# The second norm's transposes in another order, the first chunk's squares and the third chunk's loads moved up, and a padding of 512 bytes

## What is computed

```python
u = rmsnorm(h, mix_norm_g)
q, k, v, o_pre, if_pre = split(u @ w_in)
# per head, chunk by chunk, with a running state (c_st, n_st, m_st):
num = w_inter * (q @ c_st) + scores @ v          # scores = (q k^T) * exp(log_d - m_t)
den = w_inter * (q . n_st) + sum(scores)
o = _rms(num / max(|den|, exp(-m_t))) * norm_g   # head by head
h = h + (o * sigmoid(o_pre)) @ w_out
u = rmsnorm(h, ffn_norm_g)
h = h + (silu(u @ w_gate) * (u @ w_up)) @ w_down  # w_gate, w_up: 1024 x 2816
```

## Time and profile before

| | us |
|---|---|
| median of 3 runs | 2248.97 |
| lowest, highest | 2247.64, 2250.45 |
| profiled execution | 2248.88 |
| its span in the trace | 2247.2 |

### The profile page before, as it was taken

How to read it: one execution, slowest core, us unless ns; L and a number is a source line. 1 busy time by engine, 2 the same in 40 slices (tenths; PEclk the granted TensorE clock), 3 DMA queues, 4 the chain that set the end, 5 groups by cost and what they waited for, 6 DMA issues and landing times.

```text
span 2247.2 us, 29481 instructions
## 1 busy us (share of the span) xinstructions
PE 2169.3 (97%) x10440; PEld 1779.8 (79%) x10440; DVE 1459.4 (65%) x2274; ACT 922.8 (41%) x1670; POOL 282.3 (13%) x373
## 2 busy tenths in 40 slices
PE   5999989989999999999989999799899999999999
PEld 4788878878888888888868888688688888888887
DVE  8765467786656565578677644667765656656764
ACT  4433653344333333345434346433433333333443
POOL 4111111120101010100112111111210100100000
PEclk9999999999999999999999999999999999999999
DMA  4333354213232323863414334532123233257443
GB/s 142 99 113 108 105 214 141 85 47 113 99 112 89 107 95 133 300 220 113 150 61 136 99 99 146 206 132 76 55 97 108 96 102 101 93 200 239 146 128 107
DMA packets 200289, 281.56 MB, mean 125 GB/s; under 512 B 12913, under 2 KB 131697, under 8 KB 200177
## 3 DMA queue, kind: packets, MB, share of 16 engines
q1 hardware_dynamic: 171696, 183.07, 25.4%
q0 software_dynamic: 28480, 97.02, 12.3%
HBM read 197.73 MB, written 82.31 MB: 125 GB/s over the span
## 4 chain that ended last, share of the span: by engine, by line
PE 87%; DVE 7%; issue 2%; DMA 2%; ACT 2%; SPq 0%; POOL 0%; DVEq 0%; ACTq 0%; POOLq 0%
PE ps L2163 13%; PE ps L2165 13%; PE ps L2166 13%; PE ps L1912 7%; PE ps L1916 6%; PE ps L1914 6%; PE ps L2209 6%; PE ps L2213 6%; PE ps L2211 6%; PE ps L1825 2%; PE ps L1826 2%; PE ps L1827 2%; PE ps L1832 1%; DMA vtc<-proj_hbm 1%; PE ps L2082 1%
## 5 line engine op out<-in xcount | busy, mean ns | idle before, releaser
L1666 DVE TENSOR_TENSOR ring<-raw_f,ring 128x512 fp32r<-128x512 f32 x308 | 211.4, 687 | 196.8 <-ACT ring L1103 196.3
L1103 ACT CAST ring<-raw_f 128x512 fp32r<-128x512 f32 x308 | 190.4, 622 | 215.4 <-PE ps L2166 200.5
L2163 PE MATMUL ps<-u_lo,ring 128*128 128x512 f32 x704 | 277.6, 394 | 0.0
L2165 PE MATMUL ps<-u_hi,ring 128*128 128x512 f32 x704 | 276.1, 392 | 0.0
L2166 PE MATMUL ps<-u_hi,ring 128*128 128x512 f32 x704 | 275.8, 392 | 0.0
L2209 PE MATMUL ps<-ring,ring 128*128 128x512 f32 x616 | 244.4, 397 | 3.0 <-DVE ring L1744 2.9
L2213 PE MATMUL ps<-ring,ring 128*128 128x512 f32 x616 | 243.5, 395 | 0.0
L2211 PE MATMUL ps<-ring,ring 128*128 128x512 f32 x616 | 243.5, 395 | 0.0
L2163 PE MATMUL ps<-t_op,ring 128*128 128x512 f32 x528 | 208.7, 395 | 6.2 <-DVE ring L1666 6.2
L2166 PE MATMUL ps<-t_op,ring 128*128 128x512 f32 x528 | 209.0, 396 | 0.0
L2165 PE MATMUL ps<-t_op,ring 128*128 128x512 f32 x528 | 208.6, 395 | 0.0
(11 more groups left out here) (219 smaller groups left out, 4263.7 us busy)
## 6 DMA issues: line engine op xcount, KB each, us to landing
...
```

The lines of the kernel that those rows point to most:

```text
L1103: nc.scalar.copy(four(ring[slot][:, 0, :]), feed_source(q, s)).then_inc(w_hi_done, 1)
L1666: nc.vector.tensor_tensor(four(ring[slot][:, 1, :]), feed_source(q, s), four(ring[slot][:, 0, :].bitcast(F32)), ALU.subtract).then_inc(w_l ...
L2163: pe.matmul(banks(bank), wh, moved(kind, 1, k), start=(fresh and k == 0), stop=False, skip_group_check=True)
L2165: pe.matmul(banks(bank), wh, moved(kind, 0, k), start=False, stop=False, skip_group_check=True)
```

## The change

Ten edits, in the order of the diff.

1. The twelve pair units of the second norm come in the order of a new list: part B and A of all pairs first, part C (T4) of all pairs last.
2. The area `r_q` gets a padding of 512 bytes in place of 128, and the third output buffer moves with it; the areas behind it (`r_a`, `r_b`, `r_c`) move by 384 bytes.
3. SP loads `vtc` and `qkc` of chunk 2 right after the gates of chunk 0, ahead of the gates of chunk 1 and of the two pieces of `w_out`; the gain comes between these.
4. POOL squares chunk 0's numerators before it waits for the last store of the projections, sets the ones and loads the first residual.
5. `split_out(1, k)`: ACT does k 0 to 3 together after the head scales of chunk 1; VectorE does four together after `add_out` in chunks 1 and 2.
6. VectorE does the sums of pair 0 ahead of `hg_low(7)`, and `add_out(7, 0)` behind units 0 and 1, `add_out(7, 1)` ahead of unit 3's low pass.
7. ACT and VectorE do the ring slots of q 4 to 6 ahead of the T4 units and the last four units between the passes of the first group.
8. The last output tile is cut 6 + 2 instead of 4 + 4 around unit 3.
9. On TensorE units 13, 14, 15 stand in the middle of q 4, 5 and 6 instead of ahead of q 4.
10. q 4 waits for 10 units, q 6 for 12, q 12 for all.

```diff
@@ -54,2 +54,5 @@
 
+SECOND_UNITS = [("B", 0), ("A", 0), ("B", 1), ("A", 1), ("B", 2), ("B", 3), ("A", 2), ("A", 3), ("C", 0), ("C", 1),
+                ("C", 2), ("C", 3)]
 GATE_DVE = (0, 0, 8, 9, 10, 11, 12, 13, 14, 18)
@@ -151,3 +154,3 @@
         r_v = region(TILES * HEADS * VW * 4)
-        r_q = region(32 * KB + P)
+        r_q = region(32 * KB + 512)
         r_a = region(16 * KB)
@@ -193,3 +196,3 @@
         num = place("num", r_c + 28 * KB, [P, HEADS, VW], F32)
-        hg_at = [r_q, r_q + 8 * KB, r_q + 24 * KB + P]
+        hg_at = [r_q, r_q + 8 * KB, r_q + 24 * KB + 512]
         hg_hi = [place(f"hg_hi{s}", at, [P, KD, P], F32R) for s, at in enumerate(hg_at)]
@@ -400,6 +403,6 @@
         def part_of(stage, n):
-            return FIRST_UNITS[n - 4][0] if stage % 2 == 0 else "BAC"[(n - 4) % 3]
+            return (SECOND_UNITS if stage % 2 else FIRST_UNITS)[n - 4][0]
 
         def pair_of(stage, n):
-            return FIRST_UNITS[n - 4][1] if stage % 2 == 0 else (n - 4) // 3
+            return (SECOND_UNITS if stage % 2 else FIRST_UNITS)[n - 4][1]
 
@@ -567,8 +570,11 @@
                 load_og(0)
+                load_vtc(2)
+                load_qkc(2)
                 load_og(1)
+                load_wo(1, 0)
                 sp.wait_ge(colt_turned, h + 1)
                 sp.dma_start(gain2[:, :], ffn_norm_g[0:1, :].partition_broadcast(P)).then_inc(gain_loaded, 16)
-                load_wo(1, 0)
                 load_wo(1, 1)
-                for c in range(2, TILES):
+                load_og(2)
+                for c in range(3, TILES):
                     load_qkc(c)
@@ -730,6 +736,2 @@
 
-                pool.wait_ge(p_stored[1], h * 384 + 384)
-                nc.gpsimd.memset(v1[1][:, :, DV:VW], 1.0).then_inc(ones_set, 1)
-                pool.wait_ge(p_fed, h * PU + PU)
-
                 def load_res(q):
@@ -740,4 +742,2 @@
 
-                load_res(0)
-
                 def squares(c):
@@ -749,3 +749,7 @@
                         .then_inc(sq_done, 1)
-                    if 1 <= c < 4:
+                    if c == 0:
+                        pool.wait_ge(p_stored[1], h * 384 + 384)
+                        nc.gpsimd.memset(v1[1][:, :, DV:VW], 1.0).then_inc(ones_set, 1)
+                        pool.wait_ge(p_fed, h * PU + PU)
+                    if c < 4:
                         load_res(c)
@@ -1075,5 +1079,5 @@
                         act.wait_ge(p_fed, h * PU + PU)
-                    if c in (1, 2):
-                        split_out(1, 4 * c - 4)
-                        split_out(1, 4 * c - 3)
+                    if c == 2:
+                        split_out(1, 4)
+                        split_out(1, 5)
                     if c >= 3:
@@ -1086,5 +1090,4 @@
                     head_rstd(c)
-                    if c in (1, 2):
-                        split_out(1, 4 * c - 2)
-                        split_out(1, 4 * c - 1)
+                    for k in ((), range(0, 4), range(6, 8))[c] if c < 3 else ():
+                        split_out(1, k)
 
@@ -1120,3 +1123,3 @@
                 feed_hi(0, 3)
-                for n in range(5, OP_UNITS):
+                for n in range(5, 10):
                     op_hi(st + 1, n)
@@ -1128,6 +1131,8 @@
 
-                first_kept(0)
-                first_kept(1)
                 feed_hi(0, 4)
+                first_kept(0)
                 feed_hi(0, 5)
+                first_kept(1)
+                op_hi(st + 1, 10)
+                op_hi(st + 1, 11)
                 feed_hi(0, 6)
@@ -1198,2 +1203,4 @@
                             feed_hi(n, q + RING)
+                            if isinstance(n, int) and n == 0 and q < 4:
+                                op_hi(st + 1, 12 + q)
                         elif not last:
@@ -1634,4 +1638,4 @@
                     if c in (1, 2):
-                        split_out(1, 4 * c - 2)
-                        split_out(1, 4 * c - 1)
+                        for k in range(4 * c - 4, 4 * c):
+                            split_out(1, k)
 
@@ -1677,2 +1681,3 @@
                 gate_heads(7)
+                sum_early(st + 1, 0)
                 hg_low(7)
@@ -1680,12 +1685,11 @@
                 add_out(6, 1)
-                sum_early(st + 1, 0)
                 sum_early(st + 1, 1)
                 norm2_rows(6)
-                add_out(7, 0)
                 op_lo(st + 1, 0)
                 op_lo(st + 1, 1)
+                add_out(7, 0)
                 sum_early(st + 1, 2)
                 op_lo(st + 1, 2)
-                op_lo(st + 1, 3)
                 add_out(7, 1)
+                op_lo(st + 1, 3)
                 op_lo(st + 1, 4)
@@ -1695,12 +1699,13 @@
                 sum_early(st + 1, 3)
-                for n in range(6, 10):
-                    op_lo(st + 1, n)
+                op_lo(st + 1, 6)
+                op_lo(st + 1, 7)
                 feed_sums(0, 2)
-                for n in range(10, 14):
-                    op_lo(st + 1, n)
+                op_lo(st + 1, 8)
                 feed_sums(0, 3)
-                for n in range(14, OP_UNITS):
-                    op_lo(st + 1, n)
-                for q in range(4, RING):
-                    feed_lo(0, q)
+                op_lo(st + 1, 9)
+                feed_lo(0, 4)
+                feed_lo(0, 5)
+                op_lo(st + 1, 10)
+                op_lo(st + 1, 11)
+                feed_lo(0, 6)
 
@@ -1797,2 +1802,4 @@
                             feed_lo(n, q + RING)
+                            if isinstance(n, int) and n == 0 and q < 4:
+                                op_lo(st + 1, 12 + q)
                         elif not last:
@@ -2136,5 +2143,5 @@
                 out_tile(7, 0, 0, KD)
-                out_tile(7, 1, 0, 4)
+                out_tile(7, 1, 0, 6)
                 turn_unit(st + 1, 3)
-                out_tile(7, 1, 4, KD)
+                out_tile(7, 1, 6, KD)
                 turn_unit(st + 1, 4)
@@ -2184,8 +2191,10 @@
                         if first and q == 4:
-                            turn_unit(st + 1, 13)
-                            turn_unit(st + 1, 14)
-                            turn_unit(st + 1, 15)
-                            pe.wait_ge(op_lo_done, (st + 1) * OP_UNITS + OP_UNITS - 2)
+                            pe.wait_ge(op_lo_done, (st + 1) * OP_UNITS + 10)
                         if first and q == 6:
-                            pe.wait_ge(op_lo_done, (st + 1) * OP_UNITS + OP_UNITS - 1)
+                            pe.wait_ge(op_lo_done, (st + 1) * OP_UNITS + 12)
+                        if first and 4 <= q < 7:
+                            feed(n, q, b, 0, 2)
+                            turn_unit(st + 1, 9 + q)
+                            feed(n, q, b, 2, 4)
+                            continue
                         if first and q == 12:
```

6 lines of the change are left out of this document (3 added, 3 removed).

## The result

The kernel after runs in 2194.68 us (median of 4 runs, 2191.05 to 2198.51), before in 2248.3: a ratio of 0.9761, with a 95% interval from 0.9742 to 0.9781. The forecast was 2216.8 us with a range from 2207 to 2229, so the direction was right, the time lies outside the range, and 22 us of gain were not foreseen. The profiled execution took 2195.8 us, its span is 2194.1.

The account below looks back on a forecast made before the run. The prediction took TensorE, busy for 2169.3 of 2247.2 us, as the bound, with only its gaps to gain. Terms of -1.6, -3.1 and -11.4 gave -16.1 us per half, -32.2 in all: 2216.8 us, range 2207 to 2229.

Parts of the forecast that it names:

- What bounds the kernel: Whole kernel: TensorE is busy for 2169.3 of 2247.2 us, so little but its gaps can be had.
- Chunk 0, POOL: Chunk 0's head rows: POOL's squares start 2.5 us earlier, the transposes 2.1; 0.5 lost to low clock; -1.6 us per half.
- Chunk 2's values: Chunk 2: the values' earlier load removes TensorE's 3.28 us wait, but VectorE limits the gain; -3.1 us per half.
- Both together: Chunk stage: the gains from POOL's earlier squares and the values' earlier load, 4.7 us per half.
- The second norm: Second norm to q = 7: reordered work removes waits of 2.70 and 3.12 us and low clock; -11.4 us per half.
- Padding: Moved areas of rings, weights and T2/T3 operands: no effect on products, 1 us either way over the program.
- Sum: Whole program: -16.1 us per half, -32.2 in all, from 2248.97 to 2216.8 us.
- the first: Rival, chunks: VectorE is the bound there too and nothing of their 4.7 us arrives; 2226 us, chance 0.12.
- second: Rival, second norm: VectorE's queue slips by new collisions with POOL, taking half of 11.4 us; 2228 us, chance 0.11.
- the fourth: Rival, q 0 to 6: the clock stays down throughout, slower than before; 2249 us and up, at most 2273, chance 0.03.
- fifth: Rival, whole change: no effect, because a load or store was late, not the order; 2245 to 2250 us, chance 0.05.
- the third: Rival, short gaps: the clock dips once or twice more per half, 1.5 to 2.6 us each; up to 2227, chance 0.07.

## Why the prediction was wrong, by its steps

**What bounds the kernel:** right. TensorE's gaps were the place to look; that the products themselves could come faster was not asked.

**Chunk 0, POOL (-1.6):** the head rows came 2.1 us earlier and the gap is 4.3, as worked out. What it is worth hangs on the values' load (alone: nothing) and on where the clock is low; on top of the loads the traces have 0.35 and 2.0 us, the medians 0.8 for both halves, where 3.2 were forecast. So this term's size is not confirmed.

**Chunk 2's values (-3.1):** right, 3.15 and 3.29 alone. VectorE is the bound as counted: 13.9 us were worked out from the end of chunk 1's outputs to the outputs of chunk 2, and the trace of after has 325.89 - (310.08 + 2.05) = 13.8.

**Both together (-4.7):** 5.9 and 5.4 without the padding, 3.8 and 3.7 with it. The difference is mostly the clock. The weights' wait of 1.85 us did stay, but in after TensorE is granted 1.2 GHz, the lower of its two levels, for 3.4 us behind it, and in the kernel without the padding it is not: there the same product lasts 0.47 us, here 0.77. (In the first half the low stretch around chunk 0's head rows is also 3.4 us there and 6.8 here.) TensorE had run at full clock before both, and the gap is the same (1.86 and 1.85), so what decides between the two is not shown. The prediction said that a gap of 1.80 alone leaves the clock up, from one row. The Trainium skill, "TensorE: Matmul & The Clock Gate", section "A second HAM failure mode: psum-queue depth-cycling", which it weighed against that and gave 0.07, tells of a kernel in which frequent short idling between groups of products made the clock go down and up; by this stretch, the trace of after agrees, once per half, and that of the kernel without the padding does not. In the second norm, where it was feared, the granted clock is 1.00 from 467.7 to 503, and there the forecast holds.

**The second norm (-11.4):** right, 11.6 and 11.5, with the waits of 1.11 (forecast 1.3) and 0.55 (0.6), none before unit 3, none before q = 4.

**Padding (0, 1 us either way): this step failed,** and it alone put the time out of the range. It compared the mean durations of products with the T2/T3 operands and with the inputs, 395 and 394 ns, and took one for moved and the other for unmoved. Both means mix slots of both areas, and the first also holds the products on T4, which is not moved, so each holds slow and fast products in about the same share (229.6 and 229.8 ns from start to start over a group of the feed); what differs is the pair, not the operand. And the bound didn't follow even so: there are 7560 products of 512 columns in the feeds, drains and projections, so 1 ns in the mean is 7.6 us, not under 1. The gain in the traces, 53.1 - 31.5 = 21.6 us, is 2.9 ns per product. The row that would have shown it is in the same trace: steps of the same feed group at 8.37 us for 36 products and 10.89 for 48.

**Sum.** 2248.97 - 32.2 = 2216.8 is nearly the time of the kernel without the padding, 2218.5, in part by differences that cancel, as said with that kernel. The rivals: the first and second (2226, 2228) did not come, the fourth and fifth neither; the third, dips of the clock among short gaps, came once per half, in the chunks. No rival was for faster than forecast, although an edit whose purpose I couldn't name stood in the diff at a price of zero.
